# Two blocks of a transformer layer in one kernel: rows turned without norming them, the token's rms factor applied to the products, the experts' end per token tile

## The reference

```python
for i in range(2):
    x = x + 0.5 * swiglu_ffn(rmsnorm(x, ffn1_norm[i]), ffn1_wi[i], ffn1_wo[i])
    u = rmsnorm(x, mix_norm[i])
    z = u @ w_in[i]      # heads of two attention branches, gates
    ...                  # mLSTM branch A, windowed attention B
    mixed = sigmoid(ga) * (hA @ w_a[i]) + sigmoid(gb) * (hB @ w_b[i])
    x = x + mixed @ w_out[i]
    x = x + 0.5 * swiglu_ffn(rmsnorm(x, ffn2_norm[i]), ffn2_wi[i], ffn2_wo[i])
    gate = sigmoid(rmsnorm(x, ple_norm[i]) @ w_ple_gate[i])
    x = x + gate * (p[i] @ w_ple[i])
```

## Time and profile before

| what | value |
|---|---|
| runs, median (lowest to highest) | 2563.04 us (2562.63 to 2565.23) |
| the profiled execution's own time | 2564.03 us |
| its span, first to last instruction | 2562.2 us |
| mean granted TensorE clock | 0.869 of 2.4 GHz |
| TensorE busy | 1976.3 us (77%), 12475 matmuls |
| VectorE busy | 889.2 us (35%) |
| ScalarE busy | 660.5 us (26%) |
| GpSimd busy | 31.0 us (1%) |
| DMA | 659.76 MB, 257 GB/s over the span |

### The profile page before, as it was taken

The page is one execution under the profiler, slowest core; times in us unless marked ns, Lnnn a source line. Parts: engine busy times, 40 slices in busy tenths (PEclk is TensorE's granted clock), DMA queues, the critical chain, the costliest instruction groups (busy, mean ns, idle before and its releaser), DMA issues.

```text
span 2562.2 us, 33209 instructions
## 1 busy us (share of the span) xinstructions
PE 1976.3 (77%) x12475; PEld 1375.3 (54%) x12475; DVE 889.2 (35%) x1221; ACT 660.5 (26%) x925; POOL 31.0 (1%) x56
## 2 busy tenths in 40 slices
PE   6896655665656565654999887899979988889997
PEld 3554211111111111111999766799869987668995
DVE  1134000000000000001665645566646656465664
ACT  2011000000000000001444443444434444434443
POOL 0000000000000000000000000000000000000000
PEclk9997878778787778677999897899989999889998
DMA  8871799999999999998455432355435544234551
GB/s 307 323 295 67 335 427 427 427 428 427 428 427 427 427 428 426 428 428 323 158 196 185 145 115 82 126 174 176 172 118 196 193 136 151 80 132 149 174 185 50
DMA packets 173475, 659.76 MB, mean 257 GB/s; under 512 B 9859, under 2 KB 106924, under 8 KB 142388
## 3 DMA queue, kind: packets, MB, share of 16 engines
q1 hardware_dynamic: 166316, 648.71, 65.3%
q10 hardware_dynamic: 6696, 7.40, 1.0%
q0 software_dynamic: 352, 2.11, 0.2%
HBM read 655.55 MB, written 2.64 MB: 257 GB/s over the span
## 4 chain that ended last, share of the span: by engine, by line
issue 91%; PE 4%; DMA 2%; POOL 1%; DVE 1%; PEldq 0%; PEld 0%; ACTq 0%; POOLq 0%; ACT 0%; SPq 0%; DVEq 0%
PE PS L1384 2%; DMA ring<-in_w_in 1%; PE PS L1622 1%; DMA arena<-in_ret_decay_bwd 1%; PE PS L1395 1%; POOL arena L524 0%; PEldq L1401 0%; DVE arena L178 0%; PE PS L1856 0%; POOL ms L524 0%; DMA mod_rows<-wide 0%; POOL head_ms L524 0%; PE PS L1417 0%; PE PS L1346 0%; POOLq L523 0%
## 5 line engine op out<-in xcount | busy, mean ns | idle before, releaser
L178 DVE TENSOR_TENSOR units<-ring,units 128x1024 fp32r<-128x1024 f32 (+2 forms) x384 | 466.4, 1215 | 357.4 <-ACT units L178 331.0
L1622 PE MATMUL PS<-hT_split,units 128*128 128x256 f32 x4416 | 549.8, 285 | 6.7 <-DVE units L178 6.6
L1622 PEld LDWEIGHTS PS<-hT_split,units 128*128 128x128 f32 x4416 | 546.2, 194 | 13.6 <-issue 6.8
L178 ACT ACTIVATE units<-ring 128x1024 fp32r<-128x1024 f32 (+2 forms) x384 | 404.0, 1052 | 546.3 <-PE PS L1622 524.9
L178 ACT ACTIVATE arena<-PS 128x256 f32<-128x256 f32 (+3 forms) x251 | 119.7, 477 | 1046.7 <-PE PS L1592 324.5
L178 DVE SCALAR_TENSOR_TENSOR arena<-arena,PS 128x256 f32<-128x256 f32 (+2 forms) x142 | 80.6, 568 | 886.2 <-ACT arena L178 543.1
L1584 PE MATMUL PS<-moe_ring,arena 128*32 128x512 f32 x1280 | 211.9, 798 | 155.2 <-DMA moe_ring<-in_w_gate_e 80.3
L1622 PE MATMUL PS<-units,hT_split 128*128 128x512 f32 (+2 forms) x1344 | 313.3, 393 | 16.3 <-DVE hT_split L178 11.0
L1622 PEld LDWEIGHTS PS<-units,hT_split 128*128 128x128 f32 x1344 | 256.5, 194 | 65.3 <-issue 11.0
L1622 PE MATMUL PS<-units,hid_split 128*128 128x512 f32 x1056 | 255.3, 391 | 0.0
L1622 PEld LDWEIGHTS PS<-units,hid_split 128*128 128x128 f32 x1056 | 193.0, 188 | 36.6
(11 more groups left out here) (184 smaller groups left out, 989.2 us busy)
## 6 DMA issues: line engine op xcount, KB each, us to landing
moe_ring<-in_w_gate_e SPq DMA_DIRECT2D x48, 2048.0 KB, 26.0
ring<-in_w_down_e SPq DMA_DIRECT2D x48, 2048.0 KB, 26.3
ring<-in_ffn_wi SPq DMA_DIRECT2D x88, 1024.0 KB, 5.4
ring<-in_w_up_e SPq DMA_DIRECT2D x32, 2048.0 KB, 26.2
moe_ring<-in_w_up_e SPq DMA_DIRECT2D x32, 2048.0 KB, 26.1
ring<-in_ffn_wo SPq DMA_DIRECT2D x44, 1024.0 KB, 4.9
ring<-in_w_in SPq DMA_DIRECT2D x40, 1024.0 KB, 5.4
ring<-in_w_gate_e SPq DMA_DIRECT2D x16, 2048.0 KB, 26.6
```

What stands on the lines that cost most here:

```text
L178: return instruction(*args, **kwargs)
L1622: passes = [mm(out, lhs[i], rhs[j], start=start and i + j == 0, stop=stop and i == 1, **flags) for i, j in ((0, 0), (0, 1), (1, 0))]
```

## The change

1. TensorE turns x itself, not hn, for ffn1, mix, ffn2 and ple. It waits for tile 0 alone, turns its first six blocks (four in ffn1), then takes tile 1; only mixed still turns hn. `norm` no longer scales rows: ScalarE squares tile 0, copies the turned blocks, squares tile 1.
2. The root goes onto the products. GpSimd makes it and a second value, times 0.25 (ffn) or 0.5 (mix, ple). Products with tokens on partitions take it as a scale of their copy, tanh or add (by one instruction for each tile). Where tokens lie on the free axis (the gate of the feed-forward, the first piece of mix), TensorE spreads the roots over all partitions by two matmuls (`row_of_roots`), VectorE copies this row and multiplies with it: in each feed-forward step the gate is multiplied before ScalarE's tanh reads it.
3. In a feed-forward step VectorE splits the down weights of step c between this multiply and the rest, no longer at the end of step c - 1.
4. At the start of a layer ScalarE and VectorE split the first two units of ffn1 before the rows, and the gain's load is issued first. The transposes of p move from ple to before ffn2.
5. The experts' end is squared, rooted, multiplied and added tile by tile; the combining product signals after tile 0 too.
6. The copy of q and k of the mLSTM branch moves from ScalarE to VectorE. Several semaphores are merged.

The diff, cut to its core ("..." marks what is left out):

```diff
@@ -540,14 +556,20 @@
+                inverse_root("mean_squares", squares_turn(name, l), ms[:, :], eps_rms, "row_roots")
+                nc.gpsimd.drain()
+                nc.gpsimd.tensor_tensor(ms_scaled[:, :], ms[:, :], scale, ALU.mult).then_inc(S["row_roots"], 1)
-                row_root("ffn1", l)
-                row_root("mix", l)
+                scaled_root("ffn1", scales[:, 0, :], l)
+                scaled_root("mix", scales[:, 1, :], l)
                 inverse_root("ms_qk", l + 1, qk_ms, eps_rms, "qk_roots")
                 inverse_root("ms_ha", l + 1, head_ms[:, :], eps_rms, "head_roots")
-                row_root("ple", l)
+                scaled_root("ffn2", scales[:, 0, :], l)
+                scaled_root("ple", scales[:, 1, :], l)
 
         used = lambda pos: pos
...
+            for t, (signal, turn) in enumerate((("combined_first", NQ), ("combined", 1 + NQ))):
+                act.wait_ge(S[signal], turn)
+                square_sum(two_banks(6 * t), t, ms_post, arena[:, 6 * D:7 * D])
...
-            def norm(name, need, values, l, also=lambda: None):
-
-                square_sums(lambda t: x[:, t, :], ms, need, values)
-                act.wait_ge(S["row_roots"], norm_turn(name, l))
-                activation(hn[:, 0, :], x[:, 0, :], ACT.Copy, scale=ms[:, 0:1]).then_inc(S["hn"], 1)
+            def square_of(t, need, values):
+
+                act.wait_ge(S[need], values[t])
+                return activation(unread_rows, x[:, t, :], ACT.Square, scale=1.0 / 32, accum_out=ms[:, t:t + 1])
+
+            def norm(name, need, values, l):
+
+                square_of(0, need, values)
+                norm_T_hi(name, l)
+                square_of(1, need, values).then_inc(S["mean_squares"], 1)
...
-                def sub(c, base, fills):
-                    act.wait_ge(S["unit_used"], base + (2 * off + gate_unit(c) + 2))
-                    activation(f_tanh[:, c % 2, :], PS[:, 4 + c % 4, 0:TOK], ACT.Tanh,
-                                 scale=0.5).then_inc(S["f_tanh"], 1)
+            def ffn_tanh(off, hidden, base, fills):
+
+                def sub(c, hidden, base, fills):
+                    act.wait_ge(S["f_gate"], hidden + (c + 1))
+                    activation(f_tanh[:, c % 2, :], f_act[:, c % 2, :], ACT.Tanh, scale=0.5).then_inc(S["f_tanh"], 1)
...
                 before = l * LAYER_UNITS
                 layer_fills = l * (LAYER_SLOTS // R * 16)
-                norm("ffn1", "x_layer", (NT * l + 1, NT * l + 2), l, lambda: program.dma_start(
-                    p_("ffn1"), a["ffn1_norm_2"][l].rearrange("(p k) -> p k", k=KT)).then_inc(S["gain_full"], 16))
+                program.dma_start(p_("ffn1"), a["ffn1_norm_2"][l].rearrange("(p k) -> p k", k=KT)).then_inc(
+                    S["gain_full"], 16)
+                gate_up_hi(OFF_FFN1, 0, before, layer_fills)
                 act.wait_ge(S["gain_full"], (l + 1) * 16)
-                norm_T_hi("ffn1", l)
...
 
                 piece_hi(0)
                 norm("mix", "x_ffn1", (2 * l + 1, 2 * l + 2), l)
-                norm_T_hi("mix", l)
                 piece_hi(1)
-                piece_done(0)
-                activation(mqkT, PS[:, 0:4, 0:TOK], ACT.Copy).then_inc(S["mqkT"], 1)
-
+                act.wait_ge(S["row_roots"], scaled_turn("mix", l))
...
+                act.wait_ge(S["pT_ps"], l + 1)
+                activation(pT, PS[:, 4, :].rearrange("p (j n) -> p j n", j=2), ACT.Copy).then_inc(S["pT"], 1)
                 norm("ffn2", "x_mix", (2 * l + 1, 2 * l + 2), l)
-                norm_T_hi("ffn2", l)
                 gate_up_hi(OFF_FFN2, 1, before, layer_fills)
...
-                for t in range(NT):
-                    stt(hn[:, t, :], PS[:, apart * t:apart * t + 2, :].rearrange("p b n -> p (b n)"), ms_post[:, t:t + 1],
-                        gate, ALU.mult, ALU.mult)
-                for t in range(NT):
-                    tt(x[:, t, :], x[:, t, :], hn[:, t, :], ALU.add).then_inc(S[signal], 1)
+                for t in range(NT):
+                    dve.wait_ge(S["mean_squares"], norm_turn(f"last{t}"))
+                    tt(hn[:, t, :], PS[:, apart * t:apart * t + 2, :].rearrange("p b n -> p (b n)"), gate, ALU.mult)
+                    dve.wait_ge(S["row_roots"], norm_turn(f"last{t}"))
+                    last = stt(x[:, t, :], hn[:, t, :], ms_post[:, t:t + 1], x[:, t, :], ALU.mult, ALU.add)
+                    last.then_inc(S[signal], 1)
...
+            def row_of_roots(turn):
+
+                dve.wait_ge(S["root_row"], turn)
+                dve.run(V.tensor_copy, root_row, PS[:, 7, 0:TOK])
...
                 def sub(c, hidden, base):
+                    act_ = f_act[:, c % 2, :]
+                    dve.wait_ge(S["unit_used"], base + (2 * off + gate_unit(c) + 2))
+                    tt(act_, PS[:, 4 + c % 4, 0:TOK], root_row, ALU.mult).then_inc(S["f_gate"], 1)
+                    down_rest(off, c, base)
                     dve.wait_ge(S["f_tanh"], hidden + (c + 1))
-                    act_ = f_act[:, c % 2, :]
-                    stt(act_, f_tanh[:, c % 2, :], 1.0, PS[:, 4 + c % 4, 0:TOK], ALU.add, ALU.mult)
+                    stt(act_, f_tanh[:, c % 2, :], 1.0, act_, ALU.add, ALU.mult)
                        ALU.subtract).then_inc(S["f_hid"], 1)
                     if c + 2 < FFN_SUBS:
                         gate_up_rest(off, c + 2, base)
-                    if c + 1 < FFN_SUBS:
-                        down_rest(off, c + 1, base)
-
-                down_rest(off, 0, base)
+
                 for b in dve.loop(FFN_PAIRS):
...
+
+            by_root = lambda t: ms_scaled[:, t:t + 1]
 
                 before = l * LAYER_UNITS
-                norm("ffn1", l)
+                gate_up_rest(OFF_FFN1, 0, before)
                 dve.wait_ge(S["gain_full"], (l + 1) * 16)
                 norm_T_rest("ffn1", l)
...
-                add_rows(0.25, "x_ffn1")
+                dve.wait_ge(S["row_roots"], scaled_turn("ffn1", l))
+                add_rows(by_root, "x_ffn1")
                 piece_rest(0, 3)
-                norm("mix", l)
                 norm_T_rest("mix", l)
                 piece_rest(1)
+                row_of_roots(3 * l + 2)
+                dve.wait_ge(S["row_roots"], scaled_turn("mix", l))
+                used_to(OFF_Z + 2)
+                tt(mqkT, PS[:, 0:4, 0:TOK], root_row.unsqueeze(1).to_broadcast([P, 4, TOK]), ALU.mult).then_inc(
+                    S["mqkT"], 1)
...
-                dve.run(V.tensor_copy, mva[:, :, :, 0:ML_DV], heads(PS[:, 2:4, :], ML_H)).then_inc(S["mva"], 1)
+                for t in range(NT):
+                    last = ts(mva[:, t, :, 0:ML_DV], PS[:, 2 + t, :].rearrange("p (h d) -> p h d", h=ML_H),
+                              ms[:, t:t + 1], None, ALU.mult)
+                last.then_inc(S["mva"], 1)
...
-            def transpose_rows(name, base, l=0, also=None):
-
-                pe.wait_ge(S["hn"], NT * (turned_turn(name, l) + 1))
-                for k in range(KT):
-                    for t in range(NT):
-                        last = nc.tensor.transpose(PS[:, base + k // 2, (k % 2) * TOK + t * P:(k % 2) * TOK + (t + 1) * P],
-                    if k % 2 == 1:
-                        last.then_inc(S["turned"], 1)
+            def transpose_rows(name, src, need, l, alone=6):
+
+                def turn(ks, t):
+                    for k in ks:
+                        last = nc.tensor.transpose(PS[:, 4 + k // 2, (k % 2) * TOK + t * P:(k % 2) * TOK + (t + 1) * P],
+                                                   src[:, t, k:D:KT], ident)
+                    return last
+
+                pe.wait_ge(S[need], NT * l + 1)
+                turn(range(0, alone), 0)
+                pe.wait_ge(S[need], NT * l + 2)
+                turn((0, 1), 1).then_inc(S["turned"], 1)
+                turn((2, 3), 1).then_inc(S["turned"], 1)
+                turn(range(alone, KT), 0)
+                turn((4, 5), 1).then_inc(S["turned"], 1)
+                turn((6, 7), 1).then_inc(S["turned"], 1)
+
+            def row_of_roots(name, l):
+
+                pe.wait_ge(S["row_roots"], norm_turn(name, l))
+                for t in range(NT):
+                    last = mm(PS[:, 7, t * P:(t + 1) * P], ms[:, t:t + 1].to_broadcast([P, P]), ident,
+                              start=True, stop=True)
+                last.then_inc(S["root_row"], 1)
 
...
                 pe.wait_ge(S["ple_full"], 32 * (l + 1))
-                pe.wait_ge(S["x_ffn2"], NT * (l + 1))
                 for j in range(2):
                 last.then_inc(S["pT_ps"], 1)
-                transpose_rows("ple", 4, l)
                 pe.wait_ge(S["pT"], l + 1)
+                transpose_rows("ffn2", x, "x_mix", l)
+                ffn(OFF_FFN2, l * 2 * FFN_SUBS + FFN_SUBS, l * LAYER_UNITS, turned_turn("ffn2", l), "ffn2")
+                transpose_rows("ple", x, "x_ffn2", l)
```

167 lines of the change are left out of this document (84 added, 83 removed).

## The result

| | before | changed |
|---|---|---|
| five runs each, median (lowest to highest) | 2565.07 us (2562.63 to 2569.51) | 2549.56 us (2545.92 to 2553.98) |
| ratio of the runs, 95% interval | | 0.994 (0.9923 to 0.9957) |
| span of the profiled execution | 2562.2 us | 2547.8 us |
| mean granted TensorE clock | 0.869 | 0.870 |
| TensorE busy | 1976.3 us | 1986.7 us |

The changed kernel is faster by 15.5 us. The forecast was 33 us (2530, range 2520 to 2543), so the direction is right and the size is half of it, outside the range. TensorE is busy 10.4 us longer with 24 matmuls more: part of the saved waiting has come back as slower work.

A forecast was written before the change was run, and what follows sets the result against it. TensorE bounds the feed-forward loop, so time is lost only where it stands still at crossings. Terms -9.4 - 7.4 - 8.8 - 10.0 + 0.6 + 2.0 = -33.0 us gave 2530.0 us, range 2520 to 2543.

The forecast's parts named there:

- The four exits of feed-forward stages: Crossings ffn1 to mix and ffn2 to ple, two layers: net 2.35 us less each, 9.4 for four.
- the 3.90: At each feed-forward exit, the product starts at A+5.51 (A: start of the add), 3.90 us less.
- the late chain: Last feed-forward step: hidden chain starts 1.55 us later behind multiply and down-weight split; last down product waits 1.3.
- The small additions: Root row in mix 0.6 us; scaled copies, output gate's tanh and gate pieces 1.0 a layer, 2.0.
- End of the experts: 10.0 less: From the experts' combining product into first-layer ffn1: chain ends at 1227.0 against 1237.07, 10.0 us less.
- The gain, which lands 3.2 us after its issue: Experts' end: ScalarE waits for the gain, issued at 1205.5, until 1208.7; each microsecond longer costs one.
- issues 1222.8: Experts' end: ScalarE finishes its DMA issues at 1222.8, after unit copies ending at 1218.0.
- Crossing into ffn1 of the second layer: 8.8 less: From A (start of the add) to the down product: 29.24 us becomes 20.4, 8.8 less.
- Unit 0 is split by A+5.4: Second layer's ffn1: unit 0, copied earlier, is split 5.4 us after A, the start of the add.
- Crossings into ffn2: 7.4 for two: First down product from A+22.46 to 3.7 us earlier (A: start of the add), 7.4 for two layers.
- The clock, taken as unchanged: Low TensorE clock behind gaps costs 2.6 us a layer before and after; bounds -5.2 and +10.4.
- rival 2: Clock stays down after crossings filled with scattered transposes, products start at half rate: 2530 + 10.4 = 2540.4 us; chance 0.12.

The follow-up runs named there:

- Experiment 2: Changed kernel with only the last step's down-weight split put back behind the step before, in each feed-forward stage: 2542.52 us, 5.3 less.
- experiment 7: Changed kernel, but TensorE waits for both row tiles before the first transpose in all crossings: 2549.25 us, 1.4 more.
- c_again: The changed kernel run once more, unaltered, giving its second profile: 2547.84 us.
- Experiments 3 and 4: Changed kernel with eleven parameter loads issued by GpSimd, not ScalarE: 2540.61 us; then also Experiment 2's split and ffn1's gain loaded early: 2535.41 us.
- Experiment 5: The second kernel of Experiments 3 and 4, with VectorE's two layers written out instead of a hardware loop: 2528.52 us, 6.9 less.
- experiment 9: Experiment 5's kernel plus fourteen thrown-away identity matmuls before w_a's product and mixed transposes awaiting both tiles: 2520.57 us; more fillers: 2518.40; 21 before w_a: 2515.36.
- experiment 1: Changed kernel and kernel before, each run again unaltered: 2547.84 us and, in a single run, 2558.38 us.

## Why the prediction was wrong in size, point by point

- **The four exits of feed-forward stages: right.** 9.4 us were said, 9.1 measured, with the 3.90 won (3.8 to 4.0), the late chain paid (TensorE idle 1.19 us, 1.3 said) and no cost inside the loop (8.50 us a step). Experiment 2 shows the late chain to be what the prediction called it. But the 3.90 were put down to transposes that start under the second add, and experiment 7 shows that these alone give 0.7 to 1.3 us; most of it comes from having no squares, root and scaled copy ahead of them.
- **The small additions: right.** "1.0 a layer" for the tanh and the gates: from the heads' transposes to the last piece 87.41 and 87.51 us against 86.37 and 86.47. (The second profile of the kernel before had 84.88 and 86.52.) That is the sum of these terms; no run took them apart. Most of the rest of the 4.4 us in that piece of the table is the clock, above all in the second layer's fourth piece (+1.67), which c_again did not have.
- **"End of the experts: 10.0 less": 4.6.** The step that failed is ScalarE's chain behind x. "The gain, which lands 3.2 us after its issue" took 5.3, and "issues 1222.8", counted as 4.8 us, held ScalarE for 6.7. The prediction had said that each microsecond that the gain takes longer costs one, and it did. Experiments 3 and 4 took both out: d0 came 3.4 us earlier (3.0 against c_again) and then 3.0 more, where 3.2 and 3.1 were expected. The remaining 1.7 us of the miss is the clock in the first down product.
- **"Crossing into ffn1 of the second layer: 8.8 less": 5.5.** "Unit 0 is split by A+5.4" was the step: it was A+8.3, because VectorE jumps back to its loop's start for 3.1 us between the add and the split. The row of the kernel before that shows it was not among those I read. Experiment 5 removed it.
- **"Crossings into ffn2: 7.4 for two": 6.2.** The model was right: d0 at A+18.8 was said, and where the clock stayed at 1.00 (second layer of c_again) it came at A+18.79. In the first profile it came at A+19.39 in both layers, 0.6 us of clock each.
- **The clock, taken as unchanged.** The bounds stated were -5.2 and +10.4, and I took 0. By the pieces it was about +7.5: 3.9 for w_a and w_out, 1.2 in the two ffn2 crossings, 1.7 in the first down product, 1.7 in the second layer's fourth piece, 1.0 in mix, less 2.0 in ple, where it came back as the lower bound had it. The products with w_a and w_out, with half of it, were in no term at all: for w_out I took a crossing whose adds do not change as unchanged, though its transposes were reordered with the others, and what slowed w_a is open. So rival 2 was right in direction, and its price was 3 us too high and in part in the wrong places: the first product of ple ran at 1.00, and those of ffn2 lost 0.6 us each, not 2.6. I gave it 0.12 and priced it as if the rest of the sum held; the miss is this rival and two wrong terms together, a case that the range did not reach.
- **The rule on transposes** (the Trainium skill, TensorE: Matmul & The Clock Gate, Part 4: PE-mode transpose): no run here tells whether transposes count, as none filled a gap with transposes alone. Plain matmuls by the identity of the same shape did hold the clock (experiment 9).
- **2.9 us before the combining product** are in the profiled difference, and mostly luck (experiment 1). By the medians the gain is 15.5, and the miss 17.5.
